# The first 64 expert slots beside the last projection units of a hybrid decoder layer, in three buffers of their own

## The reference, cut to what matters

```python
# 1024 prompt rows and 8 x 8 sample rows, width 1024, float32 throughout
proj = rms_norm(x, attn_norm) @ w_in              # 3328 columns: q 512, k 512, v 512, p_rw 1792
o_da = diff_attend(rope(q), rope(k), v, lam)      # 4 heads, causal
o_rw, wkv, shift = rwkv_time_mix(p_rw, ...)       # 8 heads of 64, a state carried over the rows
h = x + concat(o_da, o_rw) @ w_out
hn = rms_norm(h, ffn_norm)
s = einsum(hn @ wq, sub_keys)                     # 8 heads, 2 x 128 scores each
eidx, gate = top 16 of the sums of the two top 16 # 8 x 16 = 128 experts a row, of 16384
act = gelu(dot(peer_u[eidx], hn))                 # one row of 1024 per expert and row
y = rms_norm(h + sum(gate * act * peer_v[eidx]), final_norm)
```

## Time and profile before

| | us |
|---|---|
| median of three runs (3933.78 to 3940.51) | 3938.15 |
| the profiled execution | 3939.81 |
| its span | 3938.0 |
| TensorE busy | 2867.6 (73%) |
| VectorE busy | 2598.8 (66%) |
| ScalarE busy | 1289.1 (33%) |
| POOL busy | 1379.5 (35%) |

### The profile page before, as it was taken

How to read it: one execution, slowest core, us unless ns; L and a number is a source line. 1 busy time by engine, 2 the same in 40 slices (tenths; PEclk the granted TensorE clock), 3 DMA queues, 4 the chain that set the end, 5 groups by cost and what they waited for, 6 DMA issues and landing times. The chain is left out here.

```text
span 3938.0 us, 54695 instructions
## 1 busy us (share of the span) xinstructions
PE 2867.6 (73%) x20366; PEld 1337.4 (34%) x20366; DVE 2598.8 (66%) x5836; ACT 1289.1 (33%) x3597; POOL 1379.5 (35%) x1190
## 2 busy tenths in 40 slices
PE   6899999775677576766766776677676758766565
PEld 3654454342224232322332243224222315421111
DVE  2422456398668848884987598668866776446954
ACT  1311211234333424342434334433433224332232
POOL 1000000244344434443444343434333456543453
PEclk9999999887778787878777777788787667777655
DMA  8534524799999999999999999999999999999998
GB/s 306 200 142 167 193 73 166 300 420 420 422 419 412 412 422 410 418 399 420 413 416 403 419 412 415 388 419 412 392 410 392 371 351 413 408 392 422 417 407 348
DMA packets 254826, 1431.66 MB, mean 364 GB/s; under 512 B 27520, under 2 KB 45456, under 8 KB 110304
## 3 DMA queue, kind: packets, MB, share of 16 engines
q0 software_dynamic: 163232, 1162.26, 72.4%
q1 hardware_dynamic: 91328, 265.89, 17.8%
HBM read 1373.21 MB, written 54.85 MB: 363 GB/s over the span
## 5 line engine op out<-in xcount | busy, mean ns | idle before, releaser
L1005 POOL DMA_INDIRECT pe_buf<-in_experts,pe_idx x1088 | 1294.3, 1190 | 2438.3 <-PE pe_psO L1424 1641.8
L2273 DVE CUSTOM_DVE_ANT_0 pe_buf<-pe_buf,pe_hnR 128x1024 f32<-128x1024 f32 x1088 | 1316.5, 1223 | 706.7 <-DMA pe_buf<-in_experts,pe_idx 670.9
L1424 PE MATMUL pe_psO<-pe_buf,pe_Z 128*32 128x256 f32 x8704 | 842.6, 484 | 639.6 <-ACT pe_Z L1701 615.0
L1695 ACT ACTIVATE pe_gelu<-pe_dot 128x1 f32<-128x1 f32 x1088 | 219.2, 201 | 1640.8 <-DVE pe_dot L2273 1590.9
L1424 PEld LDWEIGHTS pe_psO<-pe_buf,pe_Z 128*32 128x32 f32 x8704 | 214.5, 123 | 1305.5 <-ACT pe_Z L1701 1011.7
L1406 PE MATMUL pe_psH<-pe_hn,pe_pick 128*128 128x512 f32 x544 | 415.4, 855 | 54.2 <-ACT pe_hnR L1677 51.4
L1038 PE MATMUL ip_B<-ip_w,ip_xT 128*128 128x512 f32 (+1 forms) x1008 | 433.0, 580 | 17.6 <-DMA ip_w<-in_w_in 17.6
L1701 ACT ACTIVATE pe_Z<-pe_gl,pe_gelu 128x8 f32<-128x8 f32 x1088 | 327.3, 301 | 43.4 <-issue 0.5
L1372 PE MATMUL pe_B<-op_wkr,pe_mix 128*128 128x512 f32 (+1 forms) x576 | 271.1, 615 | 9.1 <-DMA op_wkr<-scratch_wk_rows 7.7
L1038 PEld LDWEIGHTS ip_B<-ip_w,ip_xT 128*128 128x128 f32 x1008 | 190.7, 195 | 214.3 <-issue 208.8
L1406 PEld LDWEIGHTS pe_psH<-pe_hn,pe_pick 128*128 128x128 f32 x544 | 108.8, 246 | 185.1 <-ACT pe_hnR L1677 93.7
(11 more groups left out here) (344 smaller groups left out, 3573.8 us busy)
## 6 DMA issues: line engine op xcount, KB each, us to landing
op_wkr<-scratch_wk_rows SPq DMA_DIRECT2D x36, 2048.0 KB
ip_w<-in_w_in SPq DMA_DIRECT2D x18, 2048.0 KB, 9.4
op_w<-in_w_out SPq DMA_DIRECT2D x9, 2560.0 KB
pe_buf<-in_experts,pe_idx POOLq DMA_INDIRECT x1088
op_w<-in_w_out SPq DMA_DIRECT2D x9, 1024.0 KB
ip_w<-in_peer_wq SPq DMA_DIRECT2D x4, 2048.0 KB, 11.2
scratch_wk_rows<-wk_wkc SPq DMA_DIRECT2D x16, 512.0 KB, 5.8
tm_ps<-scratch_moved_rows SPq DMA_DIRECT2D x8, 896.0 KB
```

The costliest lines, as they stand in the source:

```text
L1005: pool.indirect_dma_start(buf[b][:], None, T["experts"], bass.IndirectOffsetOnAxis(ap=idx[:, t % 2, h * NJ + j:h * NJ + j + 1], axis=0)).t ...
L1424: last = nc.tensor.matmul(psO[32 * x:32 * x + 32, j // 4, :], Z[:, n % NZ, 24 - 8 * turn:56 - 8 * turn], buf[n % NBUF][:, D + x * QUART:D ...
L1695: nc.scalar.activation(gelu[:, col:col + 1], dot[:, col:col + 1], ACT.Gelu_apprx_tanh).then_inc(f["gelu_done"], 1)
L2273: nc.vector.tensor_tensor_reduce(buf[b][:, 0:D], buf[b][:, 0:D], hnR[:, n // PH % 2, :], 1.0, 0.0, ALU.mult, ALU.add, dot[:, n % (NBUF):n ...
```

## The change: what it does

1. `FILL` gets a stage more. Tile 0's front now stands beside 92 projection steps (to unit 19). Then 48 steps (units 20 to 39) beside tile 0's choice and, after a gap, the first 12 steps of tile 1's front. Then the last 49 steps (units 40 to 62) beside the rest of tile 1's front (127 steps) and slots 0 to 63, each as two steps of cost 1.0: the slot, and ScalarE's gate. These slots have v_sum one slot late.
2. Slots 0 to 65 use three new buffers (9 to 11) only; from 66 on all twelve, until the new ones go: buffer 9 after slot 65, buffer 10 after slot 239, buffer 11 after slot 495. They lie where the keys and values of tiles 2 to 7 will be, for which keys and values now lie together tile by tile (`kv`). SP's load of the values of tiles 2, 4 and 6 waits until the buffer there has been used for the last time.
3. Units from 40 on use the one bank `psW`, since `psO` and `psH`, which share their banks with `ipB`, belong to the slots. TensorE waits before each until the one before is taken out.
4. The front of tile 2 and the choice of tile 1 stand in slots 64 to 127 (2 to 4 steps a slot), not 0 to 127. From slot 128 on the list is as before.
5. POOL's first gather waits for the sums of x and the stored folds; slot 66 waits for the stored units. SP loads the rows of tile 1 at the start of its time mixing and the hidden rows of tile 0 in its choice. Some semaphores are joined.

```diff
+IP_A, IP_B = IP.index(("unit", 2 * NG + 6, 0)), IP.index(("unit", 5 * NG + 5, 0))
+ALONE = IP[IP_B][1]
+NEXT_A, GAP = 12, 18
+FILL_SLOTS = 64
+EARLY = FILL_SLOTS + 2
+EXTRA = 3
+EXTRA_UNTIL = (EARLY, 2 * 128 - 16, 4 * 128 - 16)
 FILL = (((("ip", (0, IP_FIRST)),),),
-        ((("ip", (IP_FIRST, IP_HALF)),), (("gap", 4), ("tm", 0), ("at", 0), ("op", 0))),
-        ((("ip", (IP_HALF, IP_STEPS)),), (("tm", 1), ("at", 1), ("op", 1)), (("topk", 0),)))
+        ((("ip", (IP_FIRST, IP_A)),), (("gap", 4), ("tm", 0), ("at", 0), ("op", 0))),
+        ((("ip", (IP_A, IP_B)),), (("gap", GAP), ("next", (0, NEXT_A))), (("topk", 0),)),
+        ((("ip", (IP_B, IP_STEPS)),), (("next", (NEXT_A, None)),), (("early", (0, FILL_SLOTS)),)))
...
+def buffer_order(total):
+    last, order, before = [-1] * (NBUF + EXTRA), [], []
+    for n in range(total):
+        free = [NBUF + i for i in range(EXTRA) if n < EXTRA_UNTIL[i]] + (list(range(NBUF)) if n >= EARLY else [])
+        b = min(free, key=lambda i: last[i])
...
+        def early(lo, hi):
+            for n in range(lo, hi):
+                slot(n)
+                yield
+                if late is not None:
+                    late(n)
+                yield
...
-        for n in range(TOTAL):
+        for n in range(FILL_SLOTS, TOTAL):
...
+    def evicted(eng, units):
+        if rotated_of(units):
+            eng.wait_ge(ip["rotated"], rotated_of(units))
+        eng.wait_ge(ip["copied"], copied_of(units))
...
+        def unit_bank(g):
+            return ipB[:, bank_of(g), :] if g < ALONE else psW[:]
...
+                        if t in (2, 4, 6):
+                            sp.wait_ge(f["v_used"], 1 + max(n for n in range(TOTAL) if home[n] == NBUF + t // 2 - 1))
...
+                if n == 0:
+                    pool.wait_ge(ip["summed"], NT)
+                    for i in range(2):
+                        pool.wait_ge(wk_stored[i], 16 * PH)
+                if n == EARLY:
                     for i in range(2):
                         pool.wait_ge(ip_stored[i], stored_of(NU, i))
...
-                if n >= NBUF:
-                    pool.wait_ge(f["v_used"], n - NBUF + 1)
+                if before[n] >= 0:
+                    pool.wait_ge(f["v_used"], before[n] + 1)
...
+                            elif g == ALONE:
+                                pe.wait_ge(c["gate_ready"], 1)
+                            elif g > ALONE:
+                                evicted(pe, g)
...
+                if 0 < n < FILL_SLOTS:
+                    v_sum(n - 1)
-                if n >= SUM_LAG:
+                if n >= FILL_SLOTS + SUM_LAG - 1:
                     v_sum(n - SUM_LAG)
```

More of the change, by code:

```diff
@@ L12 @@
+import itertools
 from contextlib import ExitStack
@@ L229, in steps_of @@
         return arg[1] - arg[0]
+    if stage == "next":
+        return sum(steps_of(i) for i in NEXT) - arg[0] if arg[1] is None else arg[1] - arg[0]
+    if stage == "early":
+        return 2 * (arg[1] - arg[0])
     if stage == "at":
@@ L295, in peer @@
     plan = pulls()
+    home, before = buffer_order(TOTAL)
+    uses = [home[:n + 1].count(home[n]) for n in range(TOTAL)]
     FIRST_IN, CONSTS_IN, TM_CONSTS_IN = 2, 7, 15
@@ L306, in topk_pulls, with run @@
     def topk_pulls(t, k):
-        first = TOPK_FROM if t < LAST - 1 else TOPK_FROM_LAST
+        first = FILL_SLOTS + TOPK_FROM if t == 0 else TOPK_FROM if t < LAST - 1 else TOPK_FROM_LAST
         n = TOPK_TO - first
         return min(max(k + 1 - first, 0), n) * TOPK_STEPS // n - min(max(k - first, 0), n) * TOPK_STEPS // n
-    def run(slot, stage):
+    def run(slot, stage, late=None):
+        def early(lo, hi):
[5 more added lines that the diff above has]
+                yield
         def through(items):
             for kind, arg in items:
-                yield from range(arg) if kind == "gap" else stage[kind](arg)
+                if kind == "next":
+                    yield from itertools.islice(following, steps_of((kind, arg)))
+                elif kind == "early":
+                    yield from early(*arg)
+                else:
+                    yield from range(arg) if kind == "gap" else stage[kind](arg)
+        following = through(NEXT)
         for streams in FILL:
@@ L325, in run @@
                     raise ValueError("steps are left over")
+        if next(following, "end") != "end":
+            raise ValueError("steps are left over")
         front, choice = through([item for window in DURING for item in window]), None
-        for n in range(TOTAL):
+        for n in range(FILL_SLOTS, TOTAL):
             t, k = n // PER, n % PER
-            if k == 0 and t < LAST:
+            if (k == 0 or n == FILL_SLOTS) and t < LAST:
                 choice = stage["topk"](t + 1)
@@ L453, in peer @@
             ip_x = e.sb("x", [P, D])
+        buf = [m.sb(f"buf{b}", [P, 2 * D]) for b in range(NBUF)]
+        hnR = m.sb("hnR", [P, 2, D])
+        hn = m.sb("hn", [P, D])
+        with ExitStack() as early:
+            e = Mem(nc, early, "ip")
             ip_rope = e.sb("rope", [P, MOST, 4, 32])
@@ L859, in topk @@
             def topk(t):
-                for _ in range(TOPK_STEPS):
+                for k in range(TOPK_STEPS):
+                    if t == 0 and k == 2:
+                        load_hn(0)
                     yield
```

101 lines of the change are left out of this document (54 added, 47 removed).

## The result

The changed kernel takes 3968.68 us (median, 3957.61 to 3970.71) against 3938.15 before: ratio 1.008, 95% interval 1.0063 to 1.0097. It is slower by 30 us. The forecast was 3911 us, faster. The profiled execution took 3968.68 us too, with a span of 3966.8.

A forecast was written before the change was run, and what follows sets the result against it. TensorE bounds the fill, DMA the slots after it. Fill end 744 + 54 + 20 + 23 + 22 = 863, plus 235 gives slot 128 at 1098 (before 1122.7); less 4 later: 3911 us. Forecast's own range 3893 to 3932, overall 3855 to 3975.

The forecast's parts named there:

- (a): Fill, TensorE: v_sum (35 us) and repeat_hn (19 us) for the 64 early slots add 54 us, which nothing hides.
- (b): Fill: units, folds and fronts mixed anew, tile 0's front beside 92 projection steps, not 134; 20 us of stall, bounds 0 and 30.
- (c): Last stage of the fill: three buffers for the early slots, so late gathers hold engines; 23 us, bounds 0 and 45.
- a sign of a slower rival: Last stage of the fill: product waits on gathers above 60 us would point to the slower rivals.
- (d): Last stage of the fill: one bank instead of three for 23 units; TensorE waits, 22 us, bounds 0 and 55.
- End of the fill: Fill ends at 863 us: 744 plus 54, 20, 23 and 22 us.
- The squeezed window: Slots 64 to 127, with all of tile 2's front and tile 1's choice: 235 us, bounds 207 and 265.
- After slot 128: Later windows, DMA-bound, have 11 or 10 buffers for 9: a gain of 4 us, at most 10.
- hidden stalls: Fill grows by TensorE's 54 us and only 20 us of stalls, window takes 220 us: 3851 us; chance 0.18.
- VectorE takes the gain back: Slots 64 to 127 take 260 us, VectorE being dense there: 3936 us, no change; chance 0.16.
- One bank and the clock: Units 41 to 62 wait for the bank and start on the lower clock: 81 us for 22, 3985 us; chance 0.20.
- Three buffers set the pace: Early slots in the fill: a buffer round takes 18 us in place of 12, fill ends at 957, 4005 us; chance 0.04.

## Why the prediction was wrong, step by step

- **(a) slot work on TensorE, 54 us.** Somewhat low. In 490 to 866 us v_sum takes 41.6 us (I said 35) and the repeats 21.5 (19), together 63. I had taken half of a run of 16 records (0.54 us) for a slot; eight records by themselves take 0.64, and 64 x 0.64 = 41.
- **(b) the new mixing, 20 us.** 8 to 13 by the run with no early slots. Inside its bounds, the value taken too high. The run also has the moved loads in it.
- **(c) three buffers, 23 us.** Not measured by itself. VectorE waits 131.1 us for gathers in the last stage, over the 60 that I had named as a sign of a slower rival; but TensorE waits only 21.0 for the Z that depends on it, so the sign was badly chosen, for VectorE is not what bounds there. The 21.0 us lie near my 23, which no run separates. With three gathers in flight a slot takes 8.5 us from issue to product (median of slots 1 to 63). The estimate of 4.4 us by the Trainium skill ("DMA: Bandwidth & Descriptors", Anatomy of one DMA, the SWDGE path), by which (c) would have vanished, is not borne out by these 8.5 us.
- **(d) one bank, 22 us.** Right: 17 to 20 by the run that has only this.
- **End of the fill, 863 us.** Right in sum, and in part by luck: the product of slot 64 starts at 866.1. TensorE's busy time grew by 752.2 (windows of after up to 866 us) - 678.8 (of before up to 755.6) = 73.4 us, of which 63 are (a), where I had 54; its idle time grew by 113.8 - 76.8 = 37, where I had 65 in (b) to (d). The two misses cancel for the most part. The first gather leaves at 492.65, not between 550 and 580. My 573 was 863 - 290, which took the stage's busy time for its length; with the 335 us that I gave for the stage itself it is 528, and the stage took 354 from the first product on. From 870.92 on POOL issues eleven gathers in a row; nine were forecast.
- **The squeezed window, 235 us, bounds 207 to 265: the step that failed.** It measured 293, 58 over the forecast and 28 over the upper bound. With 3 us at the fill's end, and 6.8 us won later for 4, 58 + 3 - 3 = 58 is the whole of the distance from 3911 to 3969. VectorE's sum was right: 198, and the profile has 198.1. TensorE's was low, 184 for 199.6, and so was DMA's, 207 for 240 (0.82 x 293), but VectorE waits only 9.7 us for gathers in the window and TensorE 5.2 for a load. No term comes near 293. What failed first was the rule to join them, "a tenth or more of hand-over losses" (a hand-over is a result of one engine that another waits for). I had split the window into halves with different limits and let each end at the greater of its sums. The trace shows shorter stretches in which one engine is full and the others stand, and losses of 95 us (293 - 198) on VectorE, of which 78 in waits for TensorE or ScalarE. For most of these 78 us TensorE is at work, from 962 to 997 us at half the clock.
- **After slot 128, 4 us of gain.** 6.8 by the profile, near the number, but not shown to come from what I named. With nine buffers the squeezed kernel gets 6.4 us back too, and with twelve buffers and no squeeze slots 128 to 511 take 0.3 us less than before.

The rivals: *hidden stalls* is out, since the fill took all of its terms. *VectorE takes the gain back* named the right window with too small a price (260) and partly the wrong cause: the choice, VectorE's own load, is 18 of the 82 us that the squeeze costs by itself. Its place fits best of the four. *One bank and the clock* had the right sign, but its place, units 41 to 62, is not where the time went, and the run with one bank alone gives a quarter of its price. *Three buffers set the pace* is not what happened: TensorE is busy 312 of the 354 us and waits 21.0 for the gated columns. But a buffer's round was 16.5 us (353 / 64 x 3), nearer to that rival's 18 than to my 12. The result lies inside the range by a path that I had no rival for, and the range did not hold the two outer rivals themselves (3851 and 3985). A rival of the kind "front 2 in half the slots becomes a chain of its own" could have been priced: the front's time mixing and output beside half of the slots leave VectorE two or three products (3 us) to cover a chain that takes TensorE 13 us at full clock and 19 at half.

What stays open: how the 64 us that the front costs, with the choice spread, divide between the state's hand-overs (23.8 us waited), the tail (24.7) and the rest, and how much of them is TensorE's lower clock, which no run changes by itself. The runs separate only the choice; moving the front's end thins out all of its steps.

## What to carry to other kernels

When steps of an in-order list are moved into fewer slots, the sum for each engine does not give the window's length; look at every hand-over between engines in the trace of before, and count how much other work stands between its two ends after the move. In this case that count, and not a sum, had the answer: three products for six beside the state's chain. A transfer-bound window can give up transfers only as long as its other work still fits under what is left of them: here 32 early slots paid, 48 broke even until the tail was moved, and 64 lost.

## What the runs showed of the hardware

- TensorE at 41 of 50 us busy (950 to 1000 us) with a granted clock of 0.56, so mostly on the 1.2 GHz level: small products (64x64 and 128x64) behind waits of 5.6 and 1.4 us. From 976.8 to 996.1 it is busy 19.27 of 19.3 us at 0.50; in the kernel before the same pass of the chain runs 13.21 of 13.3 us at 1.00. In the last stage of the fill the clock is 0.93, and 0.97 before. The chain under which VectorE waits is thus longer exactly where it is exposed. The rule of the Trainium skill ("TensorE: Matmul & The Clock Gate", Part 1), by which activity releases the clock, agrees with the fall behind the wait. It does not account for 0.50 over 19.3 us without a gap, and there the measurement decides.
- A byte does not always cost the same DMA time. At 420 GB/s the share is 1.01 in the earlier trace rows, 416 GB/s for a full share. In the last stage of after 288 GB/s take 0.78 (369) and in the squeezed window 312 take 0.82 (380). Which transfers, or which mixture of them, make the difference is not shown. My 207 us for DMA was thus nearer to 240 (0.82 x 293).
